# Logits of four banded attention items as three one-pass products of high and low parts, with the item loops of three engines written out

## The chip, the cores and the metric

The kernel runs on one core of a Trainium2 chip. The metric is the device time of one execution in microseconds; the median of three runs is taken. A profiled execution gives, beside its own time, the span from the first to the last instruction that the hardware profiler saw.

## What is computed

Two transformer blocks over 512 tokens of width 2048, in float32. The first block projects its input to three attention branches and gates: sparse attention over the best 128 keys by an index score ("A", 6 heads of 128), banded attention over a window of 128 keys with a learned bias and a sink ("B", 12 query heads of 64 over 2 key heads), and attention to 256 memory tokens ("C", 4 heads of 128). The second block has dilated and neighbourhood attention. Most of the time goes into projections. The change touches branch B only. Cut to what matters:

```python
def sliding_window_attention(q, k, v, sinks, bias_tab):
    # blocks of 128 queries see the block before and their own: 256 keys
    kband, vband = band(k), band(v)
    logits = jnp.einsum('bnqhgd,bnkhd->bnhgqk', qb, kband).astype(jnp.float32) * (dh ** -0.5)
    ...
    valid = (dist >= 0) & (dist < WINDOW) & (key_pos >= 0)
    logits = jnp.where(valid[None, :, None, None], logits + bias.astype(jnp.float32), -jnp.inf)
    ...
    p = jax.nn.softmax(jnp.concatenate([logits, sink], axis=-1), axis=-1)[..., :-1]
    out = jnp.einsum('bnhgqk,bnkhd->bnqhgd', p.astype(v.dtype), vband)
```

## The kernel before

The kernel is written engine by engine. Each engine has its own program, in an order set by hand, and they meet at counting semaphores only.

**Weights.** All large projections run through one stream of weight chunks of 1 MB, two to a group of 256 output columns. SyncE loads chunk c into `w_raw[c % 2]`; ScalarE copies it to `w_hi` in the type float32r (L442, `split_hi`); VectorE subtracts to get `w_lo` (L447, `split_lo`); TensorE then makes each product as three one-pass matmuls, high by high, low by high and high by low (`mm3`, L458 to L460). The activations stand ready as high and low parts (`act_a`, `act_b`).

**Items.** Attention of the first block is cut into 16 items that ride on the groups of the mix gates, one item to a group: items 2 to 7 are B (two heads each), 8 to 11 are C, 12 to 17 are A (one head each). In `mix_item`, TensorE first computes the item's logits (`logits`, `qk`), then runs the group's four half chunks (`gemm_part`), and after the first of them the products with the values of the item before (`values`, `pv`). VectorE scales the logits, adds the bias, finds the maxima (`soft_a`, L2248 to L2255), normalises the probabilities (`soft_b`), turns them in 32x32 blocks (`flip1`), splits both weight chunks, and between them picks the next best keys for branch A (`pick`, L2226 and L2231). In a B item it picks twice, after the second split and at the end of the item. ScalarE computes the exponentials, the high parts of the chunks and the tanh of the gate that leaves the banks of the group (`mix_out`, L1564). GpSimd issues the loads of the next item (`load_item`: `qb`, `kb`, `vb`, `gb`, then the bias), the turned probabilities and the stores.

**Logits.** For a B item, `qk` makes for each of four query blocks and each of two heads a product of 64 rows, 128 query columns and 256 keys (128 keys in the last block, k = 3, which has no block before it), in full float32, L1009. The heads lie on the partition halves 0 to 63 and 64 to 127 and are issued in turn, into different PSUM banks. For the items in `SPLIT_ITEMS` (8 to 15) the inputs are first split like the weights: `logits_hi` on ScalarE copies `qb` and `kb` to `q1_hi` and `k1_hi`, and `logits_lo` on VectorE writes `q1_lo` and `k1_lo` (L2329, L2330) and counts up `tl_s`, for which TensorE waits ahead of the item's logits. Both stand in the item before, behind its second weight split; on VectorE also behind the first of the two picks. Their products are then three matmuls (L1019), except for blocks 128 keys wide, which stay whole. `idx_units` (L956), ahead of the items, has the same shape as a B item's logits in three one-pass products: two halves of 64 rows in turn, three parts, with 512, 384 and 256 columns.

**Loops.** The B items of TensorE are written out for items 2 and 3 and then stand in a loop of two trips (`pe.Fori(1, 3)`, items 4 to 7). ScalarE has items 2 to 5 in a loop of two trips and 6 and 7 written out; VectorE has items 4 and 5 in a loop of one trip. C and A items are written out on all three.

Of the kernel before, what the change touches and what calls it, by code (L numbers as in the profile page):

```python
# [25 lines left out]
P = 128  # L26
D, T, MEM = 2048, 512, 256
# [110 lines left out]
def build_kernel(nc, wst, xt_in, mem_in, par_in, con_in, pos_in, tab1_in, tab2_in, rpb_in, lng_in, lnb_in, out):  # L138
# [25 lines left out]
    with ctx:  # L164
# [11 lines left out]
        def sem(name):  # L176
# [51 lines left out]
        q1_hi, q1_lo, k1_hi, k1_lo = [[sb_at(f"{name}{i}", [P, T], RB + 32 * KB + 2 * KB * (2 * n + i), F32R) for i in range(2)]  # L228
                                      for n, name in enumerate(("q1_hi", "q1_lo", "k1_hi", "k1_lo"))]
# [133 lines left out]
        th_s, tt_s, tl_s = sem("x_normed_and_w_sums"), sem("x_and_idx_query_hi"), sem("x_and_idx_query_lo")  # L363
        IQ0 = KT + 1
        IT0 = IQ0 + 8
        SPLIT_ITEMS = range(8, 16)
        key_width = lambda it: MEM if it < 12 else T
        items_loaded = lambda it: 32 * (it - it % 2)
        pb_s, pe_s, brow_out = sem("bias_psum_and_w_part_used"), sem("bias_copied_and_first_quarter_copied"), sem("brow_out")
        sp_v, sp_h, sp_l = sem("special_chain"), sem("latent_hi"), sem("latent_lo")  # L370
# [24 lines left out]
        s_ready, l_ready, m_ready = sem("logits_psum"), sem("logits_ready"), sem("max_ready")  # L395
        e_ready, p_ready, flip1_ready = sem("exp_ready"), sem("prob_ready"), sem("prob_flipped")
        half_done = sem("first_head_done")
# [93 lines left out]
        def tb_of(k):  # L491
            return TB - 1 - k
# [11 lines left out]
        def logit1(kind, k, e=0):  # L504

            return bank[2 + 2 * (k // 2) + e] if kind == "B" else bank[2 + k]
# [168 lines left out]
        def _(pe):  # L675
# [85 lines left out]
            for c in range(C_X, C_X + 4):  # L761
                chunk_ready(pe, c)
                for kt in range(4):
                    pe.wait_ge(tl_s, 4 * (c - C_X) + kt + 1)
                    last = wide_kt(c, kt, act_a, TB, (4, 5, 6, 7))
# [23 lines left out]
            for kt in range(2):  # L789
                for b in range(TB):  # L790
                    last = pe.transpose(bank[4 + kt][:, b * P:(b + 1) * P], ckv_n[:, b, kt * P:(kt + 1) * P], ident)
# [5 lines left out]
            for kind in range(2):  # L797
                chunk_ready(pe, C_KVUP + kind)
                for b in range(TB):
# [6 lines left out]
                    for half in range(2):  # L806
                        for kt in range(2):
                            last = mm3(pe, bank[KV_BANK[u % 2] + half][:, 0:384], ckv_t[0][:, kt, b * P:(b + 1) * P],
                                       ckv_t[1][:, kt, b * P:(b + 1) * P], wt(w_hi[kind], kt, half * 384, 384, A_W),
                                       wt(w_lo[kind], kt, half * 384, 384, A_W), start=(kt == 0), stop=(kt == 1))  # L810
                    last.then_inc(chunk_used if b == TB - 1 else kv_psum, 1)
                if kind == 0:
                    for b in range(TB):
                        last = pe.transpose(bank[4][:, 80 * b:80 * b + 80], ik_f[:, b * P:(b + 1) * P], ident[0:80, 0:80])
# [187 lines left out]
            def qk(kind, it, k, q, kk):  # L1002

                tb = tb_of(k)
                if kind == "B":
                    c0 = BAND0(k)
                    for e in range(2):
                        half = slice(64 * e, 64 * e + 64)
                        pe.matmul(logit1(kind, k, e)[:, 256 * (k % 2) + c0:256 * (k % 2) + 256], q[half, tb * P:(tb + 1) * P],  # L1009
                                  kk[half, (tb - 1) * P + c0:(tb + 1) * P], start=True, stop=True)\  # L1010
                            .then_inc((half_done, s_ready)[e], 1)
                else:
                    w = width_of(kind, k)
                    parts = ((q, kk),)
                    if it in SPLIT_ITEMS and w > P:
                        qh, ql, kh, kl = (t[it % 2] for t in (q1_hi, q1_lo, k1_hi, k1_lo))
                        parts = ((qh, kh), (ql, kh), (qh, kl))
                    for n, (l, r) in enumerate(parts):
                        last = pe.matmul(logit1(kind, k)[:, 0:w], l[:, tb * P:(tb + 1) * P], r[:, 0:w],  # L1019
                                         start=(n == 0), stop=(n + 1 == len(parts)))  # L1020
                    last.then_inc(s_ready, 1)
# [38 lines left out]
            def mix_item(kind, it0, i, par, before):  # L1060

                it = 2 * i + (it0 + par)
                g = 2 * i + (G_MIX + 8 + it0 - 2 + par)
                pe.wait_ge(it_loaded[par], 64 * i + 32 * it0)
                if kind != "B" and it in SPLIT_ITEMS:
                    pe.wait_ge(tl_s, IT0 + it - 7)
                logits(kind, it, par)
                for hs in range(4):
                    gemm_part(g, hs, act_a)
                    if hs == 0 and before:  # L1070
                        values(before, it - 1, 1 - par)
# [3 lines left out]
            for kind, it0, n in (("B", 2, ITEMS_B), ("C", 8, ITEMS_C), ("A", 12, ITEMS_A)):  # L1075
                mix_item(kind, it0, 0, 0, before)
                mix_item(kind, it0, 0, 1, kind)
                if kind == "B":
                    with pe.Fori(1, n // 2) as i:
                        for par in range(2):  # L1080
                            mix_item(kind, it0, i, par, kind)
                else:
                    for i in range(1, n // 2):
                        for par in range(2):
                            mix_item(kind, it0, i, par, kind)
                before = kind
            values("A", 17, 1)

# [218 lines left out]
            for b in range(TB):  # L1307
# [3 lines left out]
                for n in range(4):  # L1311
                    pe.matmul(dst[:, n * P:(n + 1) * P], xw[1][:, n, b * P:(b + 1) * P], ident,
                              start=(n == 0), stop=False, is_transpose=True, skip_group_check=True)
                for c in range(4):
                    if b == 0:
                        chunk_ready(pe, 2 * G_OUT2 + 12 + c)
                    for kt in range(CK // 2):
                        k = CK // 2 * c + kt
# [9 lines left out]
        def _(act):  # L1328
# [323 lines left out]
            def mix_item(kind, it0, i, par, last=False, following=None):  # L1652

                it = 2 * i + (it0 + par)
                g = 2 * i + (G_MIX + 6 + it0 + par)
                for hs in range(4):
                    if hs == 0:
                        split_hi(act, 2 * g + 1, 1)
                    att_act(kind, it, hs, params[:, bass.ds(4 * i + (PAR["sink"][0] + 2 * par), 2)] if kind == "B" else None)
                    if hs == 2:  # L1660
                        split_hi(act, 2 * g + 2, 0)
                        if following in SPLIT_ITEMS:
                            logits_hi(following)
                if last:
                    act.wait_ge(l_ready, 72)
                    for p in range(2):
                        part_hi(PARTS_1, p, 1)
                mix_out(g, 2 * i + (6 + it0 + par), par)

            for kind, it0, n in (("B", 2, ITEMS_B), ("C", 8, ITEMS_C), ("A", 12, ITEMS_A)):  # L1670
                if kind == "B":
                    with act.Fori(0, 2) as i:
                        for par in range(2):
                            mix_item(kind, it0, i, par)
                for i in range(2 if kind == "B" else 0, n // 2):
                    for par in range(2):
                        it = 2 * i + it0 + par
                        mix_item(kind, it0, i, par, last=(it == 17), following=it + 1)
# [125 lines left out]
        def _(dve):  # L1804
# [519 lines left out]
            def logits_lo(it):  # L2324

                par, w = it % 2, key_width(it)
                dve.wait_ge(it_loaded[par], items_loaded(it))
                dve.wait_ge(tt_s, IT0 + it - 7)
                dve.tensor_tensor(q1_lo[par][:], qb1[par][:], q1_hi[par][:].bitcast(F32), ALU.subtract)  # L2329
                dve.tensor_tensor(k1_lo[par][:, 0:w], kb1[par][:, 0:w], k1_hi[par][:, 0:w].bitcast(F32), ALU.subtract)\  # L2330
                    .then_inc(tl_s, 1)
# [31 lines left out]
            for kind, it0, n in (("B", 2, ITEMS_B), ("C", 8, ITEMS_C), ("A", 12, ITEMS_A)):  # L2363
                if kind == "B":
                    dve.wait_ge(rt_s, 3)
                    dve.wait_ge(va, 1)
                    dve.reciprocal(rq[:], ssq_q[:]).then_inc(rq_s, 1)
                    dve.wait_ge(rq_s, 2)
                    dve.wait_ge(cz_s, 3)
                    dve.memset(flip_1[1][:], 0.0)  # L2370
                    dve.sem_inc(topk_s, 1)
                if kind == "A":

                    dve.wait_ge(topk_s, 97)
                    for tb in range(1, TB):
                        w = P * (tb + 1)
                        last = dve.tensor_scalar(score[:, tb, 0:w], score[:, tb, 0:w], -3.2e38, NEG, ALU.is_gt, ALU.mult)
                    last.then_inc(topk_s, 1)
                    dve.wait_ge(topk_s, 98)
                for par in range(2):  # L2380
                    mix_item(kind, it0, 0, par, gate=(kind != "B" or par), following=it0 + par + 1)
                if kind == "B":
                    with dve.Fori(1, 2) as i:
                        for par in range(2):
                            mix_item(kind, it0, i, par)
                for i in range(2 if kind == "B" else 1, n // 2):
                    for par in range(2):
                        mix_item(kind, it0, i, par, following=2 * i + it0 + par + 1)

# [765 lines left out]
```

## Time and profile before

| | |
|---|---|
| time, median of 3 runs | 2454.0 us (2453.28 to 2454.55) |
| time of the profiled execution | 2453.05 us |
| its span, first to last instruction | 2451.5 us |
| TensorE busy | 2439.3 us |
| VectorE, ScalarE, GpSimd busy | 1520.4, 840.1, 683.8 us |
| stretch of the B items (items 2 to 7) | 721.76 to 873.63 us |
| mean granted TensorE clock | 0.999 |

The times are microseconds from the span's start. Busy time of TensorE counts matmul records, whose ends overlap the next one's start; how long a piece of TensorE's work really holds it is read from starts: the start of the next piece less its own. One full float32 matmul of the program shows as two matmul records.

### The profile page before, as it was taken

To read this page: it belongs to the slowest core of one execution; us is meant where nothing else is said; L and a number is where in the kernel's file an instruction comes from. 1 tells how busy PE (TensorE), PEld (TensorE's weight loads), DVE (VectorE), ACT (ScalarE), POOL (GpSimd) and SP (SyncE) were. 2 spreads that over 40 slices of the span, in tenths; PEclk is the share of its full clock that TensorE was granted. 3 is DMA by queue.
4 is the path that set the end of the run, shared out by engine and by line. 5 is a ranking of instruction groups with operands and counts; after the bars stand their busy time and mean duration, and the time that the engine had idled before them with its cause. 6 is when DMAs were issued, how large, how long until landed. Compare 5 with 4: busy or idle time off the path is not lost.

```text
span 2451.5 us, 36158 instructions
## 1 busy us (share of the span) xinstructions
PE 2439.3 (100%) x13712; PEld 2086.8 (85%) x13712; DVE 1520.4 (62%) x2529; ACT 840.1 (34%) x1281; POOL 683.8 (28%) x867
## 2 busy tenths in 40 slices
PE   9999999999999999999999999999999999999998
PEld 7798999999978888888888888888888888888886
DVE  5676878898779876556554433555565546555535
ACT  7322445545453433323212222232232323223220
POOL 0313556666412232321001320212122423333100
PEclk9999999999999999999999999999999999999999
DMA  7759333433457666777444444666656555546622
GB/s 289 223 176 299 113 127 126 135 130 130 147 165 239 237 234 238 247 252 264 162 164 155 147 144 118 216 199 200 198 187 209 187 163 158 181 158 211 246 88 103
DMA packets 102149, 451.48 MB, mean 184 GB/s; under 512 B 18006, under 2 KB 18070, under 8 KB 73926
## 3 DMA queue, kind: packets, MB, share of 16 engines
q1 hardware_dynamic: 38712, 241.58, 28.5%
q0 software_dynamic: 63312, 208.20, 26.6%
q8 instruction: 82, 1.34, 0.2%
q14 instruction: 43, 0.35, 0.0%
HBM read 350.94 MB, written 100.26 MB: 184 GB/s over the span
## 4 chain that ended last, share of the span: by engine, by line
PE 97%; DVE 2%; DMA 1%; SPq 0%; ACT 0%; issue 0%; DVEq 0%
PE bank L458 22%; PE bank L459 22%; PE bank L460 22%; PE bank L875 16%; PE bank L1264 5%; PE bank L1182 2%; PE bank L1320 2%; PE bank L1161 2%; PE bank L1044 1%; PE bank L1019 1%; DMA w_raw<-wst 1%; PE bank L956 1%; PE bank L1039 0%; PE bank L1009 0%; DVE w_lo L447 0%; DVE k_nat L1810 0%
## 5 line engine op out<-in xcount | busy, mean ns | idle before, releaser
L447 DVE TENSOR_TENSOR w_lo<-w_raw,w_hi 128x2048 fp32r<-128x2048 f32 x164 | 375.8, 2291 | 332.3 <-ACT w_hi L442 330.0
L458 PE MATMUL bank<-act_b,w_hi 128*128 128x512 f32 x1280 | 500.8, 391 | 0.0
L459 PE MATMUL bank<-act_b,w_lo 128*128 128x512 f32 x1280 | 498.3, 389 | 0.0
L460 PE MATMUL bank<-act_b,w_hi 128*128 128x512 f32 x1280 | 498.0, 389 | 0.0
L442 ACT ACTIVATE w_hi<-w_raw 128x2048 fp32r<-128x2048 f32 x163 | 311.8, 1913 | 454.2 <-PE bank L460 365.1
L458 PE MATMUL bank<-act_a,w_hi 128*128 128x512 f32 (+2 forms) x1032 | 398.8, 386 | 0.3 <-DVE w_lo L447 0.3
L459 PE MATMUL bank<-act_a,w_lo 128*128 128x512 f32 (+2 forms) x1032 | 394.8, 383 | 0.0
L460 PE MATMUL bank<-act_a,w_hi 128*128 128x512 f32 (+2 forms) x1032 | 394.7, 382 | 0.0
L458 PEld LDWEIGHTS bank<-act_b,w_hi 128*128 128x128 f32 x1280 | 240.2, 188 | 53.6 <-issue 4.1
L460 PEld LDWEIGHTS bank<-act_b,w_hi 128*128 128x128 f32 x1280 | 240.3, 188 | 50.3
L459 PEld LDWEIGHTS bank<-act_b,w_lo 128*128 128x128 f32 x1280 | 240.3, 188 | 49.1
L875 PE MATMUL bank<-t_xh,pt_w 128*128 128x256 f32 x1280 | 232.1, 283 | 0.0
L458 PEld LDWEIGHTS bank<-act_a,w_hi 128*128 128x128 f32 (+1 forms) x1032 | 193.4, 187 | 38.2 <-issue 2.1
L460 PEld LDWEIGHTS bank<-act_a,w_hi 128*128 128x128 f32 (+1 forms) x1032 | 193.4, 187 | 36.2
L459 PEld LDWEIGHTS bank<-act_a,w_lo 128*128 128x128 f32 (+1 forms) x1032 | 193.5, 188 | 34.0
L875 PEld LDWEIGHTS bank<-t_xh,pt_w 128*128 128x128 f32 x1280 | 199.7, 192 | 0.0
L875 PE MATMUL bank<-act_a,pt_w 128*128 128x256 f32 x1440 | 181.5, 283 | 0.0
L875 PE MATMUL bank<-t_xl,pt_w 128*128 128x256 f32 x640 | 181.1, 283 | 0.0
L875 PEld LDWEIGHTS bank<-act_a,pt_w 128*128 128x128 f32 x1440 | 176.2, 192 | 3.0 <-DVE pt_w L2110 2.1
L2110 DVE TENSOR_TENSOR pt_w<-s_sum,pt_w 128x512 fp32r<-128x512 f32 x160 | 155.2, 983 | 36.9 <-ACT pt_w L1333 36.3
L2789 POOL TENSOR_TENSOR s_sum<-w_raw 128x512 f32<-128x512 f32 x80 | 119.8, 1508 | 109.2 <-DMA w_raw<-wst 63.9
L1333 ACT ACTIVATE pt_w<-s_sum 128x512 fp32r<-128x512 f32 x160 | 100.6, 630 | 94.1 <-PE bank L875 79.8
(376 smaller groups left out, 3352.9 us busy)
## 6 DMA issues: line engine op xcount, KB each, us to landing
w_raw<-wst SPq DMA_DIRECT2D x210, 1024.0 KB, 5.0
prob_t<-flip_d POOLq DMA_DIRECT2D x64, 512.0 KB, 4.7
flip_d<-flip POOLq DMA_DIRECT2D x56, 512.0 KB, 4.2
mix_d<-stage POOLq DMA_DIRECT2D x24, 512.0 KB, 3.3
mixg<-mix_d POOLq DMA_DIRECT2D x8, 1536.0 KB, 6.8
prob_tk<-flip_d POOLq DMA_DIRECT2D x32, 256.0 KB, 5.8
flip_d<-flip_a POOLq DMA_DIRECT2D x16, 512.0 KB, 2.9
b<-rows_2d POOLq DMA_DIRECT2D x16, 448.0 KB, 10.3
```

The costliest lines, as they stand in the source:

```text
L442: act.activation(w_hi[s][:], w_raw[s][:], ACT.Copy).then_inc(hi_ready, 1)
L447: dve.tensor_tensor(w_lo[s][:], w_raw[s][:], w_hi[s][:].bitcast(F32), ALU.subtract).then_inc(lo_ready, 1)
L458: pe.matmul(out_ap, l_hi, r_hi, start=start, stop=False)
L459: pe.matmul(out_ap, l_lo, r_hi, start=False, stop=False)
L460: return pe.matmul(out_ap, l_hi, r_lo, start=False, stop=stop)
L875: last = pe.matmul(quarter(g, i), pt_w[i][l][:, j, :], x_part(c, i, r, j), start=(i % 2 == 0 and c == 0 and j == 0 and m == 0), stop=(c == ...
L1161: ins = pe.matmul(logit_bank(kind, step, cc, e)[:, off:off + w], q[half, c * P:(c + 1) * P], keys(k, half), start=(n == 0), stop=(n == 2))
L1182: last = pe.matmul(bank[O_BANK][64 * e:64 * e + 64, c * P:(c + 1) * P], v[:, b, 64 * e:64 * e + 64], turned[:, e, b], start=(b == 0), stop ...
L1264: last = pe.matmul(bank[4 * s + b][:], act_b[l][:, k, b * P:(b + 1) * P], wt(r[c % 2], kt, 0, 2 * GC, 2 * GC), start=(k == 0 and n == 0), ...
L1333: return act.activation(dst, src, ACT.Copy, **kw)
L2110: dve.tensor_tensor(pt_w[i][1][:], w_part(c, i), pt_w[i][0][:].bitcast(F32), ALU.subtract)\
L2789: pool.tensor_tensor(dst[:], l, r, op).then_inc(ws_s, 1)
```

## The change

Items 4 to 7, the last four of B, join `SPLIT_ITEMS`. Their logits are made of three one-pass products instead of a full one, for the 256 and the 128 wide blocks; the two heads stay interleaved inside each part. `logits_hi` and `logits_lo` now also run for them in items 3 to 6, with 512 columns of keys, and TensorE waits for `tl_s` ahead of their logits. Since the items in a loop would no longer be alike, the B loops of TensorE, ScalarE and VectorE are written out.

```diff
-        SPLIT_ITEMS = range(8, 16)
-        key_width = lambda it: MEM if it < 12 else T
+        SPLIT_ITEMS = range(4, 16)
+        key_width = lambda it: MEM if 8 <= it < 12 else T
...
                     c0 = BAND0(k)
-                    for e in range(2):
-                        half = slice(64 * e, 64 * e + 64)
-                        pe.matmul(logit1(kind, k, e)[:, 256 * (k % 2) + c0:256 * (k % 2) + 256], q[half, tb * P:(tb + 1) * P],
-                                  kk[half, (tb - 1) * P + c0:(tb + 1) * P], start=True, stop=True)\
-                            .then_inc((half_done, s_ready)[e], 1)
+                    parts = ((q, kk),)
+                    if it in SPLIT_ITEMS:
+                        qh, ql, kh, kl = (t[it % 2] for t in (q1_hi, q1_lo, k1_hi, k1_lo))
+                        parts = ((qh, kh), (ql, kh), (qh, kl))
+                    for n, (l, r) in enumerate(parts):
+                        for e in range(2):
+                            half = slice(64 * e, 64 * e + 64)
+                            last = pe.matmul(logit1(kind, k, e)[:, 256 * (k % 2) + c0:256 * (k % 2) + 256],
+                                             l[half, tb * P:(tb + 1) * P], r[half, (tb - 1) * P + c0:(tb + 1) * P],
+                                             start=(n == 0), stop=(n + 1 == len(parts)))
+                            if n + 1 == len(parts):
+                                last.then_inc((half_done, s_ready)[e], 1)
...
-                if kind != "B" and it in SPLIT_ITEMS:
-                    pe.wait_ge(tl_s, IT0 + it - 7)
+                if it in SPLIT_ITEMS:
+                    pe.wait_ge(tl_s, IT0 + it - 3)
...
-                if kind == "B":
-                    with pe.Fori(1, n // 2) as i:
-                        for par in range(2):
-                            mix_item(kind, it0, i, par, kind)
-                else:
-                    for i in range(1, n // 2):
-                        for par in range(2):
-                            mix_item(kind, it0, i, par, kind)
+                for i in range(1, n // 2):
+                    for par in range(2):
+                        mix_item(kind, it0, i, par, kind)
...
-                if kind == "B":
-                    with act.Fori(0, 2) as i:
-                        for par in range(2):
-                            mix_item(kind, it0, i, par)
-                for i in range(2 if kind == "B" else 0, n // 2):
+                for i in range(n // 2):
...
-                dve.wait_ge(tt_s, IT0 + it - 7)
+                dve.wait_ge(tt_s, IT0 + it - 3)
...
-                if kind == "B":
-                    with dve.Fori(1, 2) as i:
-                        for par in range(2):
-                            mix_item(kind, it0, i, par)
-                for i in range(2 if kind == "B" else 1, n // 2):
+                for i in range(1, n // 2):
```

## Rows read from the trace of the kernel before

**Rows 1.** The page: span, TensorE's busy line, the chain by engine.
```profile
span 2451.5 us, 36158 instructions
...
PE 2439.3 (100%) x13712; PEld 2086.8 (85%) x13712; DVE 1520.4 (62%) x2529; ACT 840.1 (34%) x1281; POOL 683.8 (28%) x867
...
PE 97%; DVE 2%; DMA 1%; SPq 0%; ACT 0%; issue 0%; DVEq 0%
```
**Rows 2.** The waits of PE: us in total, times, longest.
```profile
PE bank L743 <- POOL warm L2705: 1.6, 1, 1.6
PE bank L458 <- DVE w_lo L1862: 0.8, 1, 0.8
PE bank L458 <- DVE w_lo L447: 0.3, 1, 0.3
```
**Rows 3.** PE's timeline where items 3, 4, 5, 7 and 8 begin: start, length.
```profile
745.46 1.79 PE L1009 MATMUL bank<-kb,qb 64*128 64x256 f32 x16
...
770.79 0.39 PE L460 MATMUL bank<-act_a,w_hi 128*128 128x512 f32 x1
771.11 1.79 PE L1009 MATMUL bank<-kb,qb 64*128 64x256 f32 x16
772.83 0.50 PE L458 MATMUL bank<-act_a,w_hi 128*128 128x512 f32 x1
...
796.77 1.79 PE L1009 MATMUL bank<-kb,qb 64*128 64x256 f32 x16
...
848.07 1.79 PE L1009 MATMUL bank<-kb,qb 64*128 64x256 f32 x16
...
873.63 0.28 PE L1019 MATMUL bank<-k_hi,q_hi 128*128 128x256 f32 x1
```
**Rows 4.** PE's timeline over one `idx_units`, one-pass products on two halves.
```profile
667.73 0.50 PE L956 MATMUL bank<-ik_part,iq_hi 64*128 64x512 f32 x2
668.07 0.40 PE L956 MATMUL bank<-ik_part,iq_lo 64*128 64x512 f32 x2
668.30 0.57 PE L956 MATMUL bank<-ik_part,iq_hi 64*128 64x512 f32 x4
...
669.19 0.28 PE L956 MATMUL bank<-ik_part,iq_lo 64*128 64x256 f32 x2
669.31 0.28 PE L956 MATMUL bank<-ik_part,iq_hi 64*128 64x256 f32 x2
669.52 0.50 PE L458 MATMUL bank<-act_a,w_hi 128*128 128x512 f32 x1
```
**Rows 5.** PE's timeline over eight records with two moving columns each.
```profile
51.63 0.95 PE L723 MATMUL bank<-con,row_sums 128*128 128x2 f32 x8
52.44 0.49 PE L458 MATMUL bank<-hi_m,mem_t 128*128 128x512 f32 x1
```
**Rows 6.** DVE's timeline: end of item 3, item 4, then the split in item 7.
```profile
770.80 0.68 DVE L2231 MATCH_REPLACE8 score<-top,score 128x512 f32<-128x512 f32 x1
772.44 0.88 DVE L2248 SCALAR_TENSOR_TENSOR prob<-bank,rq,bb 128x256 f32<-128x256 f32 x2 [0.97 <-PE bank L1009]
...
775.86 2.28 DVE L447 TENSOR_TENSOR w_lo<-w_raw,w_hi 128x2048 fp32r<-128x2048 f32 x1
...
792.95 0.68 DVE L2231 MATCH_REPLACE8 score<-top,score 128x512 f32<-128x512 f32 x1
...
796.32 0.67 DVE L2231 MATCH_REPLACE8 score<-top,score 128x512 f32<-128x512 f32 x1
...
870.50 0.68 DVE L2329 TENSOR_TENSOR q_lo<-qb,q_hi 128x512 fp32r<-128x512 f32 x1
871.10 0.42 DVE L2330 TENSOR_TENSOR k_lo<-kb,k_hi 128x256 fp32r<-128x256 f32 x1
```
**Rows 7.** ACT's timeline: end of item 4, then the copies in item 7.
```profile
786.14 1.91 ACT L442 ACTIVATE w_hi<-w_raw 128x2048 fp32r<-128x2048 f32 x1
797.07 1.26 ACT L1564 ACTIVATE stage<-bank,half_b 128x512 f32<-128x512 f32 x2 [9.03 <-PE bank L460]
...
865.59 0.64 ACT L1333 ACTIVATE q_hi<-qb 128x512 fp32r<-128x512 f32 x1 [0.58 <-DMA gb<-g_d]
```
**Rows 8.** POOL's load of `gb` in item 4, and the landing of all eight.
```profile
784.36 0.56 POOL L2835 DMA_DIRECT2D gb<-g_d x1
...
DMA to landing us min/median/max: 3.2/4.8/6.8
```

## The prediction

> **What bounds the kernel now.** I read the head of the page first. TensorE is busy for 2439.3 of 2451.5 us, and the chain that ended last is 97% TensorE [rows 1]. The next view is TensorE's list of waits, since only a wait that ends there can give time back: the longest is 1.6 us, for the warm-up tile, and the longest on the weight stream are 0.8 and 0.3 us [rows 2]. So nothing that another engine does faster helps, and nothing that it does slower hurts as long as TensorE never has to wait. Third, TensorE's timeline at the start of each B item [rows 3]. Item 4 starts its logits at 771.11 and its first weight product at 772.83: the logits hold TensorE for 1.72 us of an item of 25.66 us (771.11 to 796.77). That piece, in four items, is all that the change can shorten: 6.9 us, or 0.28% of the time, if it cost nothing at all. Last, the timelines of VectorE, ScalarE and GpSimd in item 4, for the room that the new copies and subtractions have [rows 6 to 8]. A difference within 0.2%, 4.9 us, can hardly be told from no change for this kernel.
>
> **The logits on TensorE.** Before, an item issues 8 full products, 16 records, in 1.72 us [rows 3]. After, it issues 24 one-pass products: three parts for each of three 256-wide pairs and one 128-wide pair. Their shape, two halves of 64 rows in turn, stands in the trace in `idx_units`, so I price them by starts there [rows 4]. The first 512-wide pair takes 0.34 us (667.73 to 668.07), the second 0.23, so entering the 64-row shape costs 0.11. A 256-wide pair takes 0.12 (669.19 to 669.31). The last 256-wide pair to the next weight product takes 0.21 (669.31 to 669.52), so leaving costs 0.09. An item's logits then take 0.11 + 9 x 0.12 + 3x + 0.09 = 1.28 + 3x, where x is the price of a 128-wide one-pass pair. No row shows that one. Below, half a 256-wide pair gives 0.06. Above, the full product bounds it: 1.72 less 0.11 and 0.09 is 1.52 us for three 256-wide pairs and one 128-wide, shared by width 0.22 for the 128-wide; a one-pass product should not be dearer than the full one. Between them lie eight records that stream two columns each and still take 0.81 us, 0.10 each (51.63 to 52.44) [rows 5]; what they share with the new pass is the 128 columns of weights loaded for each. A pass that streams 128 columns is nearest to that row, so I take x = 0.10.
>
> That makes 1.28 + 0.30 = 1.58 us, 0.14 less than before; over four items 0.56 us are saved. With x = 0.06 it is 1.46 and 1.04 saved; with x = 0.22 it is 1.94 and 0.88 lost.
>
> The 0.10 is a float32 row, and what it shows is a floor that does not come from the columns streamed [rows 5]. The Trainium skill, "TensorE: Matmul & The Clock Gate", section "LDWEIGHTS (loading the stationary operand)", says that a load takes the stationary columns over 1.2 in nanoseconds, whatever the rows: 107 ns for 128. By that the sum would be an estimated 0.48 us saved, and the row agrees. The same page of the Trainium skill gives, in "Back-to-back issue gap", about 81 ns for a stream of loads and matmuls at 128 columns; by that an estimated 0.80 us would be saved. No run here shows which holds for a one-pass product.
>
> **The copies and subtractions.** ScalarE gets two copies in each of items 3 to 6. The 512-wide one takes 0.64 us [rows 7], so both together 1.28. In item 4 it is done with the second weight split at 788.05 (786.14 + 1.91) and next needed at 797.07, when TensorE releases the bank after 9.03 idle [rows 7]; that tanh is what queues behind the copies, and TensorE needs its banks. The copies also wait for the item's loads. The last of these, `gb`, is issued at 784.36, and the slowest of the eight landed after 6.8 us [rows 8]: at the latest 791.16, copies done at 792.44. That leaves 4.6 us ahead of the tanh. Price nothing, covered by that idle time. No load is moved past another.
>
> VectorE gets two subtractions of 0.60 us each by starts (870.50 to 871.10) [rows 6], 1.20 an item, after the first pick, which ends at 793.63 (792.95 + 0.68): after the copies even for the slowest landing, so VectorE does not wait for ScalarE. They end 23.72 us into the item; TensorE wants them at 25.52, its new period (25.66 less 0.14). Spare: 1.80 us. But VectorE is nearly full itself. In item 4 it works from 772.44 to 796.99 (796.32 + 0.67), 24.55 us, and its idle time before that, 0.97, ends with TensorE's logits [rows 6]. With 1.20 more it needs 25.75 an item against 25.52, so it falls behind. Item 3 ended at 771.48 (770.80 + 0.68); 1.20 later is 772.68, so item 4 starts 0.24 late, and each item after adds 0.23: 0.47, 0.70, 0.93 at item 7. The spare shrinks from 1.80 to 1.10 for the subtraction in item 6 and to about 0.9 in item 7, whose own subtraction for item 8 was there before. No wait for TensorE. What else is late by at most 0.93 is the first weight split of an item. It ends at 778.14 in item 4 (775.86 + 2.28) [rows 6], while TensorE releases the first chunk only shortly before 786.14, when ScalarE starts the copy that waits for that [rows 7]: about 8 us of cover. C items need no second pick, so the lag ends there. If the cover were gone, TensorE would move at VectorE's pace, 25.75 against 25.66 before: at most 0.1 us lost an item, 0.4 in all. Price nothing.
>
> **The loops.** Item 3 is written out and lasts 25.65 us (745.46 to 771.11); item 4, the first in the loop, lasts 25.66; items 5 and 6 together, over the jump back, 51.30 (796.77 to 848.07) [rows 3]. So a trip of the loop costs TensorE at most 0.01 us an item, and its removal gives nothing. The price of fetching the longer code can be bounded the same way: item 3 is straight code already and is no slower. On ScalarE and VectorE the loop's cost hides behind the same TensorE period.
>
> **The sum.** The profiled execution took 2453.05 us, 1.6 of it outside the span. Less 0.56 it is 2452.5. The median of the runs shown, 2454.0, lies 0.95 above the profiled one, so set against it I expect 2453.4.
>
> **The rivals.**
> *The 128-wide pass at half the 256-wide* (x = 0.06). For it: nothing but proportion; against it, the records that stream two columns and take 0.10. 1.04 saved: 2453.0. The 81 ns of the Trainium skill's page named above would put the time between this and my forecast.
> *The 128-wide pass as dear as the full one* (x = 0.22). For it: the code before keeps 128-wide blocks whole in branch A, though that is no measurement; against it, the full product needs two records. 0.88 lost: 2454.9.
> *VectorE becomes the bound in items 4 to 7.* For it: 25.75 us of work in a 25.52 us period. Against: the lag needs to eat 1.80 us of spare at 0.23 an item. 0.4 lost: 2454.4.
> *The subtraction comes too late* (other side). TensorE waits at the head of items 4 to 7 with all its weight products queued behind. It decides when the parts come more than 1.80 us later than worked out, for instance because the loads land late. At 3.5 us later TensorE would wait about 2.1 us at each of the four items, 8.4 less 0.56: 2461.8. Against it: even the slowest landing leaves the pick, not the load, as what the subtraction follows.
> *The change does not do what it says:* the two halves no longer overlap, so each pair costs twice. 9 x 0.12 + 3 x 0.10 = 1.38 more an item, 5.5 less 0.56 in all: 2459.0. Against it: the same alternation of halves and parts in `idx_units` runs both in 0.12.
> *The loops cost more than they show*, and writing them out gives over 4.9 us: 2449.0 or less. Against it the equal items above.
>
> **How the numbers follow.** My forecast has 45%; the cheap 128-wide pass 20%; the dear one 20%; VectorE as the bound 8%; the late subtraction 3%; halves that do not overlap 2%; the loops 2%. The first four, 93%, stay within 0.2%; 5% are slower, 2% faster. The range runs from 1.04 saved on the profiled execution (2452.0) to 0.88 and 0.4 lost on the slowest run shown (2454.55 + 1.28 = 2455.8); it leaves out only the last three rivals.
>
> **What would show it.** In the profile after, items 4 to 7 should have 24 records of logits, 1.58 us from their first start to the next weight product, and an item of 25.52; 0.06 or 0.22 for the 128-wide pass would show as 1.46 or 1.94. VectorE's idle time ahead of the scaling of items 5 to 7 should be gone. TensorE's waits should have no row with `k_lo`; one there makes the spare wrong. If item 3, which keeps its full product, changed its length, the loops or something that I have not seen would be at work. A difference outside 721 to 880 us would make the argument from TensorE's pace wrong.

## The result and the profile after

The changed kernel takes 2457.14 us, the median of 22 executions (2451.35 to 2462.03); the kernel before takes 2453.76 on the same chip, 22 executions (2452.46 to 2459.57). The ratio is 1.0012, interval 1.0007 to 1.0018: 2.9 us slower by the ratio (3.4 by the medians), where 0.6 us faster was forecast, and outside the range. The medians hide a change of kind. Of the changed kernel's executions 13 of 22 lie over 2456 us, of those of before 3 of 22. So a wait that comes in some executions is looked for first, before a price that each one pays. In two of the runs further down one or two executions lie far out (3018, 5126 and 8975 us); medians, ratios and counts there leave them out.

The page's head, the chain by engine and the queue that brings the engines' programs:

```profile
span 2458.1 us, 36169 instructions
...
PE 2441.1 (99%) x13744; PEld 2088.3 (85%) x13744; DVE 1517.7 (62%) x2537; ACT 844.9 (34%) x1289; POOL 687.9 (28%) x867
...
q8 instruction: 85, 1.39, 0.2%
...
PE 93%; DMA 3%; DVE 2%; SPq 1%; issue 0%; ACT 0%; POOL 0%; DVEq 0%; POOLq 0%; ACTq 0%
```

Against [rows 1] TensorE is busy 1.8 us longer but the span grew by 6.6, and transfers have come into the chain: TensorE waits more. TensorE's waits (us in total, times, longest), to be held against [rows 2], have one entry that grew from 0.3 us to 3.6, a new one of 1.1 us (what else is new is 0.3 us or less) and none with `k_lo` or `q_lo`:

```profile
PE bank L458 <- DVE w_lo L447: 3.6, 2, 3.2
PE bank L743 <- POOL warm L2699: 1.6, 1, 1.6
PE bank L1184 <- DMA prob_t<-flip_d: 1.1, 1, 1.1
```

The first stands at 231 us, long before the B items; the second at 1555 us (1549 in the kernel before), in the second block. The code there is the same in both kernels. Where the two traces part can be added up by the same TensorE instruction in each: the changed kernel is 0.5 us late after the first loads (48 us), 5.7 late behind the wait at 231 us, 5.67 late at the start of item 4 (776.78 against 771.11 in [rows 3]), 5.08 late at the start of item 8 (878.71 against 873.63), 6.3 late behind the wait for `prob_t`, and 6.7 at the end. The changed stretch alone gave time back. In this one execution the wait at 231 us is thus the dearer, some 5.1 us against 1.3; which of the two makes the median is for the experiments.

TensorE's timeline of item 4, and the starts of items 6 to 8:

```profile
776.78 0.38 PE L1014 MATMUL bank<-k_hi,q_hi 64*128 64x256 f32 x2
777.00 0.28 PE L1014 MATMUL bank<-k_hi,q_lo 64*128 64x256 f32 x2
777.12 0.28 PE L1014 MATMUL bank<-k_lo,q_hi 64*128 64x256 f32 x2
...
777.95 0.22 PE L1014 MATMUL bank<-k_hi,q_hi 64*128 64x128 f32 x2
778.01 0.28 PE L1014 MATMUL bank<-k_hi,q_lo 64*128 64x128 f32 x2
778.12 0.27 PE L1014 MATMUL bank<-k_lo,q_hi 64*128 64x128 f32 x2
778.32 0.50 PE L458 MATMUL bank<-act_a,w_hi 128*128 128x512 f32 x1
...
827.79 0.38 PE L1014 MATMUL bank<-k_hi,q_hi 64*128 64x256 f32 x2
...
853.30 0.39 PE L1014 MATMUL bank<-k_hi,q_hi 64*128 64x256 f32 x2
...
878.71 0.28 PE L1026 MATMUL bank<-k_hi,q_hi 128*128 128x256 f32 x1
```

The logits hold TensorE for 1.54 us (776.78 to 778.32; 1.72 before), and item 6 lasts 25.51 us (827.79 to 853.30). VectorE's timeline at the scaling of item 4 and around the parts for item 5, then ScalarE's:

```profile
778.07 0.87 DVE L2246 SCALAR_TENSOR_TENSOR prob<-bank,rq,bb 128x256 f32<-128x256 f32 x2
...
799.75 0.69 DVE L2328 TENSOR_TENSOR k_lo<-kb,k_hi 128x512 fp32r<-128x512 f32 x1
...
802.93 0.68 DVE L2229 MATCH_REPLACE8 score<-top,score 128x512 f32<-128x512 f32 x1
803.52 0.87 DVE L2246 SCALAR_TENSOR_TENSOR prob<-bank,rq,bb 128x256 f32<-128x256 f32 x2
```

```profile
795.65 0.61 ACT L1335 ACTIVATE k_hi<-kb 128x512 fp32r<-128x512 f32 x1
802.39 1.27 ACT L1566 ACTIVATE stage<-bank,half_b 128x512 f32<-128x512 f32 x2 [6.12 <-PE bank L460]
```

VectorE goes from the pick into the scaling without idling, and ScalarE still has 6.12 us ahead of the tanh.

### The profile page after: what moved, and what is told of

It is laid out like the page before. It is cut to its first block, busy times and chain, and to the rows that moved or that the text cites. A ratio compares the mean times of both kernels' runs of the same rounds, so it can differ in the third digit from the quotient of the medians.

```text
span 2458.1 us, 36169 instructions
## 1 busy us (share of the span) xinstructions
PE 2441.1 (99%) x13744; PEld 2088.3 (85%) x13744; DVE 1517.7 (62%) x2537; ACT 844.9 (34%) x1289; POOL 687.9 (28%) x867
## 4 chain that ended last, share of the span: by engine, by line
PE 93%; DMA 3%; DVE 2%; SPq 1%; issue 0%; ACT 0%; POOL 0%; DVEq 0%; POOLq 0%; ACTq 0%
PE bank L458 21%; PE bank L459 21%; PE bank L460 21%; PE bank L875 16%; PE bank L1266 5%; PE bank L1184 2%; PE bank L1322 2%; PE bank L1163 1%; PE bank L1051 1%; DMA x_raw_q<-x_d 1%; PE bank L1026 1%; DMA rows_b<-rows_1b 1%; DMA raw_m<-wst 1%; PE bank L956 1%; DVE w_lo L447 1%
## 5 line engine op out<-in xcount | busy, mean ns | idle before, releaser
L447 DVE TENSOR_TENSOR w_lo<-w_raw,w_hi 128x2048 fp32r<-128x2048 f32 x164 | 381.2, 2325 | 332.2 <-ACT w_hi L442 330.0
L2108 DVE TENSOR_TENSOR pt_w<-w_raw,pt_w 128x512 fp32r<-128x512 f32 x120 | 120.8, 1052 | 26.5 <-ACT pt_w L1335 26.2
## 6 DMA issues: line engine op xcount, KB each, us to landing
b<-rows_2d POOLq DMA_DIRECT2D x16, 448.0 KB, 10.1
```

The costliest lines, as they stand in the source:

```text
L447: dve.tensor_tensor(w_lo[s][:], w_raw[s][:], w_hi[s][:].bitcast(F32), ALU.subtract).then_inc(lo_ready, 1)
L2108: dve.tensor_tensor(pt_w[i][1][:], w_part(c, i), pt_w[i][0][:].bitcast(F32), ALU.subtract)\
```

## The two new waits

**At 1555 us (1549 in the kernel before).** GpSimd's timeline, first of before, then of after (start, length, what it issues, idle time before):

```profile
1533.01 0.68 POOL L3012 DMA_DIRECT2D flip_d<-flip  x1 [2.39 <-DVE flip L2511]
...
1537.53 0.78 POOL L3023 DMA_DIRECT2D prob_t<-flip_d  x1 [1.49 <-DMA flip_d<-flip]
1538.94 0.77 POOL L3023 DMA_DIRECT2D prob_t<-flip_d  x1 [0.64 <-DMA flip_d<-flip_a]
```

```profile
1538.09 0.68 POOL L3006 DMA_DIRECT2D flip_d<-flip  x1 [2.38 <-DVE flip L2505]
...
1543.76 0.78 POOL L3017 DMA_DIRECT2D prob_t<-flip_d  x1 [2.64 <-DMA flip_d<-flip]
1544.98 0.77 POOL L3017 DMA_DIRECT2D prob_t<-flip_d  x1 [0.45 <-issue]
```

The store of the turned probabilities is waited for 1.49 us before and 2.64 after: it landed in 3.96 us there and in 5.12 here. So the second load of `prob_t` is issued 6.89 us behind the store instead of 5.93. SyncE's next 1 MB of weights comes 7.64 us behind the store in both, and GpSimd's own 448 KB loads of `rows_2d` right behind `prob_t`. With 0.96 us less of a start on them the `prob_t` load lands in 10.77 us instead of 7.19, and TensorE waits:

```profile
1555.80 0.66 PE L1184 MATMUL bank<-prob_t,v_tok_a 128*64 128x128 f32 x8 [1.09 <-DMA prob_t<-flip_d]
```

The traces of all runs below agree: issued 5.9 us behind the store this load lands in 6.4 to 8.8 us, issued 6.6 us or more behind it in 10.8 to 13.6.

What lies in the way of the store is seen when the transfers of after are looked at by queue in the stretch 1540.0 to 1540.6 us (packets, MB, share of 16 engines), and then in 1511.0 to 1512.6, where nothing else runs:

```profile
q8 instruction: 1, 0.02, 9.6%
```

```profile
DMA packets 1, 0.02 MB, mean 10 GB/s; under 512 B 0, under 2 KB 0, under 8 KB 0
...
q8 instruction: 1, 0.02, 3.7%
```

An engine's program comes in pieces of some 16 KB, one packet each, and each of these two pieces keeps one of the 16 DMA engines for 0.9 us (9.6% of 16 x 0.6; 3.7% of 16 x 1.6). Around here they follow each other every 20 to 30 us. In before, pieces fall 11.3 us ahead of the store and 18.7 behind it. In after one falls 2.1 us behind it, while the store is under way; the store takes 1.16 us longer to land.

**At 231 us.** VectorE's timeline where it takes up the first sums of `x`, in before and then in after, and the product behind them in after:

```profile
216.09 1.22 DVE L2090 TENSOR_TENSOR x_raw_t<-x_raw_q,x_raw_q 128x1024 f32<-128x1024 f32 x1 [3.02 <-DMA x_raw_q<-x_d]
```

```profile
221.95 1.23 DVE L2088 TENSOR_TENSOR x_raw_t<-x_raw_q,x_raw_q 128x1024 f32<-128x1024 f32 x1 [8.25 <-DMA x_raw_q<-x_d]
...
234.91 0.47 PE L458 MATMUL bank<-act_a,w_hi 128*128 128x512 f32 x1 [3.24 <-DVE w_lo L447]
```

From 186 to 235 us the queues are jammed (the DMA engines are 94% busy, 95% in before), and the last quarter of `x_raw_q` landed in 19.59 us instead of 14.87. All that VectorE does behind it is late, the next `w_lo` too. The table by stretches of after (start:end, length, PE busy, granted clock, DMA share, GB/s) shows what follows:

```profile
231.70:234.90 3.20, 0.00 (x0) 1.00 0.80 327
...
235.73:238.70 2.97, 2.97 (x8) 0.50 1.01 299
...
1556.00:1562.00 6.00, 6.00 (x39) 1.00 0.60 137
```

TensorE does nothing for 3.2 us, and soon after starts seven products (235.73 to 238.71; the row counts one more that was still running) at a granted clock of 0.50, its lower level of 1.2 GHz, 0.43 us apart instead of 0.23: with the products just before and behind them 1.7 us more. Behind the 1.09 us wait at 1555 us the clock stays at 1.00.

## The experiments

The theory: the changed and unrolled code moves the reads of TensorE's program, and one of them meets the store of the second block. Its rivals: the new products or copies cost more somewhere than TensorE's trace shows; the code is dearer because there is more of it; buffers in memory are placed otherwise; the jam at 186 to 235 us alone is the cause. Each kernel was timed in five rounds beside the kernel before on the same chip, with one profile. 2456 us, some 2 us over the median of before, is the mark above which executions are counted. The letters in the expectations stand for theories as they were held at the time; the one above came only behind the first eight runs, and is D there.

**The changed kernel once more.** No edit.

> The changed kernel once more, beside the kernel before on the same chip. In its first profile the four changed items were 0.5 us faster in all, and the loss was elsewhere: TensorE waited 3.2 us for a weight split at 231 us and then ran at half clock for 3.4 us, in a stretch that the change does not touch. Theory A (the written-out code makes the early transfers land later): stalls at about 231 us again, median 2 to 5 us over before. Theory B (the jam of transfers there varies from execution to execution, whatever the kernel): before and after show the same spread, medians within 1 us. Theory C (the split itself does it): like A for this run.

2455.93 us (11 executions), ratio 1.0012 (1.0002 to 1.0021). Its profile has both waits again, 3.29 us up to 234 and 2.43 up to 1557 us.

**One part of the change at a time.** The loops written out, the four items' products left in full float32:

```diff
-        SPLIT_ITEMS = range(4, 16)
-        key_width = lambda it: MEM if 8 <= it < 12 else T
+        SPLIT_ITEMS = range(8, 16)
+        key_width = lambda it: MEM if it < 12 else T
```

> Only the loops are written out, the logits of items 4 to 7 stay full float32 products. Theory A: as slow as the changed kernel plus 0.6 us, 2 to 5 us over before, with a wait at about 231 us. Theory B: as before within 1 us. Theory C: as before within 1 us.

The opposite, the three-pass products with the loops kept; `loops_kept` keeps one on each of the three engines, `pe_loop` on TensorE alone:

```diff
-                for i in range(1, n // 2):
-                    for par in range(2):
-                        mix_item(kind, it0, i, par, kind)
+                if kind == "B":
+                    with pe.Fori(1, n // 2) as i:
+                        for par in range(2):
+                            mix_item(kind, it0, i, par, kind, split=True)
...
```

> The split is made, but TensorE keeps its loop over items 4 to 7, VectorE its loop of one trip over items 4 and 5, and ScalarE a loop of one trip over items 4 and 5. Theory A: no stall at 231 us, 0.6 us faster than before. Theory B: 0.6 us faster than before, within the spread. Theory C: as slow as the changed kernel.

> The changed kernel with only TensorE's loop over items 4 to 7 kept; ScalarE and VectorE are written out. Theory A: the most code is TensorE's, so most of the loss goes: within 1 us of before; if the loss stays, it is the code of ScalarE and VectorE. Theory B: 0.6 us faster than before, within the spread. Theory C: as slow as the changed kernel.

`loops_only` took 2453.54 us, ratio 0.9997 (0.9988 to 1.0006); `loops_kept` 2453.10, 0.9995 (0.9986 to 1.0004); `pe_loop` 2453.98, 0.9998 (0.9989 to 1.0007). One of 33 executions lies over 2456. None of the profiles has a wait for `prob_t`. So neither the products and copies nor the longer code cost 3 us by themselves: only both together do. That doesn't fit a price paid for each item, and of the three theories in the expectations none fits all four runs: A wanted `loops_only` slow, C the two others, and B the changed kernel no slower than before. In these three the pieces fall 18 to 19 us ahead of the store and 11 to 16 behind it.

**Buffers elsewhere, and the kernel before with longer code.** In the changed kernel a tensor in memory is made 3 MB larger and put first, so that all others shift; in the kernel before, a loop of TensorE far from the B items is written out:

```diff
+    first_d = nc.dram_tensor("first_d", [12, 16 + 65536 + 1024], F32).ap()[:, 0:16]
...
-            with pe.Fori(1, 8) as j:
+            for j in range(1, 8):
                 up_group(j)
```

> The changed kernel with one scratch tensor in HBM made 3 MB larger (256 KB in each of 12 rows, unused) and put first, so that the others lie elsewhere in HBM; no instruction changes but for addresses. Theory A2 (where the program and its scratch tensors happen to lie decides how the transfers of 186 to 231 us interleave, which neither the loops nor the split alone changes for the worse): the share of stalled executions changes from about one in two, most likely to the one in ten of before, median 2453 to 2455. Rival A3 (it is the code of the changed kernel, not its data's place): as slow as the changed kernel, median 2455.9 to 2457.1, about half of the executions over 2457.

> The kernel before with a later loop of TensorE (seven trips of the up projections) written out, so that its program is longer by far more than the change makes it, and nothing that runs before 1100 us differs. Theory A2: may go either way; a median over 2455 with stalls at 231 us would show that the length of code that has not yet run is enough. Rival A3: as before, within 0.5 us, since none of the changed items' code is there.

The first took 2456.12 us, ratio 1.0007 (0.9998 to 1.0016), with 6 of 11 executions over 2456: where the buffers lie is not what brings them. Its one profile, at 2452.54 us, has no wait: the piece falls 1.7 us behind the store, which lands in 4.71 us, and `prob_t` is still in time. A piece in that place makes the wait likely, not certain. The second is the kernel before with other code and nothing else: 2457.03 us, ratio 1.0008 (0.9998 to 1.0019), 6 of 11 over 2456, where the kernel before on the same chip has 7 of 35. Its piece falls 2.3 us behind the store, which lands in 5.37 us. TensorE's waits in its profile begin with

```profile
PE bank L1182 <- DMA prob_t<-flip_d: 3.0, 1, 3.0
```

The kernel before has the wait of the changed one as soon as its code is longer by the right amount. Neither expectation had a wait in the second block. Both intervals alone reach 1; the trace and the counts over 2456 bear the reading.

**Less in the jam at 186 to 235 us.** The broadcast of `rows_2d` goes behind the load and the stores that follow it, in the changed kernel and in before:

```diff
             iq_store(G_IQ + 2)
-            bias_rows(rows_2d, rows_2[:])
...
             iq_store(G_IQ + 3)
+            bias_rows(rows_2d, rows_2[:])
```

> The changed kernel with the broadcast to rows_2d, 16 heads of 92 KB each, issued some 10 us later, behind the stores of kt_a, so that the last quarter of x_raw_q does not share the queues with it. If the late landing of that quarter is what starts the loss (both theories A), it lands 4 us or more earlier, TensorE's wait at 231 us and the half clock behind it go, and the median is 2452.5 to 2453.5. If the wait there is only a symptom of slow weight loads, nothing changes: 2456 to 2457.

> The same move of the rows_2d broadcast in the kernel before. It should lose only its occasional stalled executions: median 2453 to 2454, no execution over 2456. Beside the changed kernel with the same move it shows what the split alone is worth: 0.5 us.

The wait at 231 us shrank to 0.92 us in the changed kernel, but it took 2457.13 us, ratio 1.0013 (1.0004 to 1.0022), where 2452.5 to 2453.5 was expected: the profile has 2.65 us of waiting for `prob_t`, its piece 1.8 us behind the store. Before with the same edit: 2453.74, 0.9999 (0.9991 to 1.0008), with 2 of 11 over 2456 where none was expected. So the jam is not what makes the median; the wait in the second block is enough.

**The pieces moved, and nothing else.** TensorE counts up a semaphore that nobody waits for, spread over the C items' weight products: 121 times in the changed kernel, 136 times in the kernel before.

```diff
-                last = rows_t(pe, s, kts, act, (0, 1))
+                for kt in kts:
+                    last = rows_t(pe, s, [kt], act, (0, 1))
+                    if pads:
+                        for _ in range(pads.pop()):
+                            pe.sem_inc(pad_s, 1)
...
+            PADS = [121 // 56 + (p < 121 % 56) for p in range(56)]
```

> The changed kernel with 121 added semaphore increments in TensorE's program, spread over the weight products of the C items, with no other purpose than to make that program longer there. Theory D (TensorE's program is read in pieces of 16 KB by the same DMA engines; the change moves the places of these pieces against the work, and the one near 1535 us now falls 2 us behind the store of the turned probabilities and makes it late): 121 instructions move that piece some 12 us earlier, about 11 us ahead of the store as in the kernel before; the store lands in 3.9 us again, the wait at 1549 us goes, and the median falls by 1.5 to 3 us, to 2453.5 to 2455; stalls at 231 us may stay. Theory A2 in its plain form (more code is worse): as slow as the changed kernel or slower, 2456 to 2458.

> The kernel before with 136 such increments, so that the piece that it reads 11 us ahead of that store and the next, 19 us behind it, move until one falls 2 us behind the store. Theory D: the store lands in 4.7 to 5.4 us, TensorE waits 1 to 3 us at 1549 us in most executions and runs at half clock behind it, median 2456 to 2458 although nothing of the change is in it. If the place of the pieces does not matter: 2454, as before.

> The changed kernel with both: the 121 increments and the later rows_2d broadcast. If the two waits are separate, at 231 us from the jam of early transfers and at 1549 us from the piece of program, both go: median 2453.0 to 2453.6, the best of all kernels, with the 0.5 us of the split in hand, and hardly an execution over 2456.

The changed kernel, its pieces now 10.1 us ahead of the store and 19.2 behind, took 2454.1 us, ratio 0.9996 (0.9987 to 1.0005); 1 of 11 executions over 2456, the profiled one, which has the wait at 231 us (2.99) and none for `prob_t`. The kernel before, its piece moved to 2.1 us behind the store, took 2458.16, ratio 1.0015 (1.0006 to 1.0024), 9 of 11 over 2456; the kernel before on the same chip has 1 of 27. GpSimd's row of the first `prob_t` load, in `after_shift` and then in `before_shift`, has the shorter and the longer wait for the store (it landed in 3.90 and 5.19 us), and TensorE's waits in `before_shift` begin with the two lines behind:

```profile
1540.98 0.78 POOL L3024 DMA_DIRECT2D prob_t<-flip_d  x1 [1.43 <-DMA flip_d<-flip]
```

```profile
1542.01 0.78 POOL L3030 DMA_DIRECT2D prob_t<-flip_d  x1 [2.71 <-DMA flip_d<-flip]
```

```profile
PE bank L1189 <- DMA prob_t<-flip_d: 1.9, 1, 1.9
PE bank L1049 <- DMA prob_tk<-flip_d: 1.7, 1, 1.7
```

This is the two-sided test: idle instructions of one kind take the loss from the changed kernel and bring it to the one before. With the `rows_2d` broadcast later as well (`after_shift_late`) it is 2452.88 us, 0.9996 (0.9987 to 1.0005), none over 2456.

**How near is near.** The changed kernel with 40, 20 and 64 increments; only the number differs.

> The changed kernel with 40 increments in place of 121. They move the piece of program by some 4.4 us, to about 2.5 us ahead of the store of the turned probabilities: near it, but done before the store begins. Theory D: the store lands in 3.9 to 4.1 us, no wait at 1549 us, median 2453.5 to 2454.5. If it is not the meeting of the two that costs, but for instance the increments that helped by being many, the wait stays and the median is over 2455.5.

> The changed kernel with 20 increments of an unused semaphore on TensorE in the C items: the read of TensorE's program should fall about 0.1 to 0.5 us ahead of the store flip_d<-flip at 1533 us. If a read anywhere from 3 us ahead to 2.3 us behind the store delays it, the store lands in 4.7 to 5.7 us, the second load of prob_t is issued over 6.4 us after the store, TensorE waits 1 to 3 us for it, and the median is 2456 to 2458.5 us. If only a read behind the store does harm, the store lands in 3.9 to 4.1 us, no such wait comes, and the median is 2452.9 to 2454.5 us.

> The changed kernel with 64 increments: the read should fall 4.3 to 6 us ahead of the store, ahead of the load v_tok_a and of SyncE's weight load that are issued 3 us ahead of it. Either theory expects no harm from a read there: store landed in 3.9 to 4.1 us, second load of prob_t issued 5.9 us after the store, no wait for prob_t, median 2452.9 to 2454.5 us. A wait for prob_t here would mean that the place of the read is not what decides.

With 40 the piece fell 3.0 us ahead of the store. The profiled execution, 2462.7 us, waited 3.4 us for `prob_t`: the piece met the load of `v_tok_a` and the weights issued beside it (landed in 6.44 and 7.36 us, 5.63 and 4.98 in after), and the store behind them took 5.64. Yet the median is 2453.83, ratio 1.0001 (0.9992 to 1.001), and 3 of 10 executions are over 2456: the expected median came, the expected trace did not. With 20 the piece didn't move: it stayed 2.1 us behind the store. So this run repeats the changed kernel with some added work and tells nothing of a read just ahead of the store: 2458.19 us, 1.0013 (1.0004 to 1.0022), 9 of 11 over 2456, a wait of 4.0 us. With 64 it falls 5.8 us ahead, and the profile shows GpSimd and TensorE's waits as in before, but for 0.4 us for `prob_tk`:

```profile
1533.07 0.68 POOL L3013 DMA_DIRECT2D flip_d<-flip  x1 [1.83 <-DVE flip L2512]
...
1537.51 0.78 POOL L3024 DMA_DIRECT2D prob_t<-flip_d  x1 [1.41 <-DMA flip_d<-flip]
1539.00 0.77 POOL L3024 DMA_DIRECT2D prob_t<-flip_d  x1 [0.71 <-DMA flip_d<-flip_a]
```

```profile
PE bank L744 <- POOL warm L2706: 1.6, 1, 1.6
PE bank L459 <- DVE w_lo L1867: 0.8, 1, 0.8
PE bank L1056 <- DMA prob_tk<-flip_d: 0.4, 1, 0.4
```

2453.14 us, 0.9995 (0.9986 to 1.0004), none of 11 over 2456.

All kernels by where the piece falls in their one trace each (negative: ahead of the store), with their times:

```
piece at          kernels                                      executions over 2456 us
+1.7 to +2.3 us   after, again, dram_pad, late, shift_20;      55 of 88
                  before_code_pad, before_shift
-3.0 us           after_shift_40                                3 of 10
-5.8 us or        loops_only, loops_kept, pe_loop, before_late, 4 of 77
farther           after_shift, after_shift_late, after_shift_64
-11.3 / +18.7     before (beside the others, all chips)        19 of 155
```

## Why the prediction was wrong

**The step that failed is the loops'.** It said that "the price of fetching the longer code can be bounded the same way: item 3 is straight code already and is no slower", and priced it at nothing. That bound looks at the stretch where the code stands, and there it holds. What the longer program changes is the place of every read behind it: TensorE's program comes in pieces over the DMA engines that also carry the data, and the change put one onto a store of 512 KB 660 us behind the items. There TensorE waits 1.1 to 4.0 us in the profiles that have the wait, and in the longer cases a stretch at half clock behind it. The step on TensorE's pace failed with it: a difference outside 721 to 880 us was to make the argument wrong, and it does. The rival of a loss that the prediction held had it in the items.

**The size.** 0.6 us gained in the items and 2.9 lost in all leaves about 3.5 us for the rest, by the ratio. When only its code is moved, the kernel before gets 2.0 and 3.7 us slower by the ratios (`before_code_pad`, `before_shift`; 2.8 and 4.2 by the medians), so the late store can carry most or all of it. How much of the 2.9 the wait at 231 us adds is not shown.

**The steps that held.** The logits: 1.54 us where 1.58 was worked out; the three 128-wide pairs of item 4 took 0.06, 0.11 and, less 0.09 for leaving, 0.11, together 0.28 where 3 x 0.10 was taken. The choice of the row with two columns as the nearest was right for two of three, the proportional 0.06 for the first. The item: 25.51 us, worked out 25.52, and item 3 with its full product lasts 25.66 (25.65 before). The four items: 101.93 us (776.78 to 878.71) where [rows 3] give 102.52, so 0.59 saved, worked out 0.56. The copies: covered, the tanh still found 6.12 us. The subtractions: done 23.57 us into item 4 (800.35, the start of what follows them), worked out 23.72, no wait. When the piece lies away from the store the whole change comes out at 2453.14 and 2454.1 us, around the 2453.4 forecast; both ratios hold 1 in their intervals, so the gain of 0.6 us is read from the traces alone.

**A small miss.** VectorE was to fall 0.23 us behind an item. It didn't: from the scaling of one item to the next takes 25.45 us (778.07 to 803.52), under TensorE's 25.51, with no idle time in between that TensorE ends; its work in an item is thus at least 0.3 us less than the 25.75 that item 4 of the kernel before gave. Some 0.2 of that is the step from the last replacement of the first pick to the instruction behind it: 0.78 us before (792.95 to 793.73), 0.59 now that a subtraction follows (798.56 to 799.15). The idle time ahead of the scaling is gone, as forecast. By itself this would have changed nothing.

**What stays open.** The wait at 231 us, where it is 2.9 us or more, comes with a landing of over 19 us of that last `x_raw_q` quarter; in all other profiles it landed in 17.9 us or less. Of seven profiles of the changed kernel, whole but for the place of code or buffers, four show 2.9 us or more; of three of the kernel before, with its code as it was or moved, none is over 1.0, and of the three with one part of the change none over 0.62. Pieces of code lie in the jam in all of them, with no pattern that sorts the landings, and the time without a profile says little for it: `after_shift` has the wait in its profile and 10 of 11 executions under 2455. With the later broadcast it was 0.92 us and nothing in the changed kernel, but three of the seven without it show 0.6 us or less too, so that isn't settled either. Also open is how a piece between 3 us ahead of the store and 1.7 us behind it acts; no kernel put one there. Why 20 increments moved nothing is open too.

## What to carry to other kernels

In a kernel like this one, where TensorE is busy to 99% and each transfer has its time, a longer program changed the transfers far behind the new code; list the transfers whose landing something waits for, with their spare, before calling a code change free. When a local gain vanishes, align the two traces by the same instructions and look where they part, then move the code alone, with instructions that do nothing, in both kernels. A difference of 0.1% that comes from some executions only needs the spread of the times, not the median alone.

## What the hardware showed

The program of TensorE is read in single packets of about 16 KB, since added TensorE instructions moved them; the two measured above kept one DMA engine for 0.9 us each, and a store that met one behind its issue landed in 4.7 to 5.4 us instead of 3.8 to 4.1. The added increments moved the pieces by 5.1 us (40), 7.9 (64) and 12.2 (121), with some 28 us from piece to piece, and not at all with 20. The Trainium skill, "Advanced Engine Details and Errata", section "ISA Cache", gives a line of 16 KB, or 256 instructions. By that 40, 64 and 121 of 256 would be an estimated 4.4, 7.1 and 13.4 us of 28.4, the distance of the two pieces ahead of the store in after, and the traces agree to about 1.2 us; 20 would be 2.2 us, and there they do not agree.

A pair of one-pass products of 128 columns on two halves of 64 rows cost 0.06 us once and 0.11 to 0.12 us twice in a row of three, in each of the four items, where 256 columns cost 0.12.
